# A hybrid decoder layer: residual read back earlier, norm sums in four column quarters, norm factors spread by transposes, attention scores in four quadrants

## What is computed

```python
u = rmsnorm(h, norm1_g);  proj = u @ w_in            # 7 parts of 512 columns
# stick-breaking attention, 8 heads of 64:
z = einsum('bhqd,bhkd->bhqk', qb, k) * scale
log_one_minus = where(visible, log_sigmoid(-z), 0)
later = cumsum(log_one_minus, reverse=True) - log_one_minus
o_sb = where(visible, exp(log_sigmoid(z) + later), 0) @ v
o_sb = group_rmsnorm(o_sb, sb_norm_g, 8)             # mean square over each head's 64
# gated linear recurrence, 4 heads of 128, chunks of 128 tokens
o_hg = hgrn2_chunkwise(q, k, v, log_f)
o_hg = group_rmsnorm(o_hg, hg_norm_g, 4) * silu(g)
h = h + concat([o_sb, o_hg]) @ w_out                 # the residual h is x
ffn = (silu(u2 @ w_gate) * (u2 @ w_up)) @ w_down;  h = h + ffn;  rmsnorm(h)
```

## Time and profile before

| | us |
|---|---|
| median of 3 runs | 1467.88 (1467.37 to 1468.05) |
| the profiled execution's time | 1466.36 |
| its span | 1464.3 |
| TensorE busy | 1401.8 |
| VectorE busy | 738.0 |
| ScalarE busy | 440.6 |

### The profile page before, as it was taken

One profiled execution on the slowest core, in us unless ns is written; L12 is line 12 of the kernel. 1 busy time (PEld: TensorE's weight loads), 2 busy tenths in 40 slices (PEclk: granted clock), 3 DMA queues, 4 the chain that ended last, 5 costly groups with the idle time before them and its releaser, 6 DMA issues.

```text
span 1464.3 us, 20834 instructions
## 1 busy us (share of the span) xinstructions
PE 1401.8 (96%) x8732; PEld 1190.4 (81%) x8732; DVE 738.0 (50%) x1178; ACT 440.6 (30%) x770; POOL 20.3 (1%) x48
## 2 busy tenths in 40 slices
PE   5999999998999999769999999999999999999998
PEld 5898989897777777569987888888888888888886
DVE  6476677763776565812542435252533425152437
ACT  6323322223665556811432112111111112121113
POOL 3000000000000000010000000000000000000000
PEclk9999999999999999989999999999999999999999
DMA  6211111010010000040121011020201111020202
GB/s 189 58 30 30 30 30 53 22 44 0 1 59 1 30 2 30 1 158 30 58 73 58 29 58 58 29 87 0 86 23 63 31 55 57 29 86 0 86 0 115
DMA packets 61194, 68.78 MB, mean 47 GB/s; under 512 B 1584, under 2 KB 54832, under 8 KB 61120
## 3 DMA queue, kind: packets, MB, share of 16 engines
q1 hardware_dynamic: 59408, 61.94, 13.2%
q0 software_dynamic: 1712, 5.78, 1.1%
HBM read 63.51 MB, written 4.19 MB: 46 GB/s over the span
## 4 chain that ended last, share of the span: by engine, by line
PE 91%; ACT 5%; DMA 1%; issue 1%; DVE 1%; POOL 0%; ACTq 0%; DVEq 0%; POOLq 0%
PE ps L268 18%; PE ps L269 18%; PE ps L270 18%; PE ps L1542 16%; PE ps L936 3%; PE ps L917 2%; PE ps L280 2%; PE ps L282 2%; PE ps L281 2%; PE ps L901 2%; PE ps L549 2%; PE ps L384 1%; DMA h_res<-in_x_dram 1%; ACT bv L503 1%; ACT beta L1029 1%
## 5 line engine op out<-in xcount | busy, mean ns | idle before, releaser
L268 PE MATMUL ps<-a_hi,w_hi 128*128 128x512 f32 (+2 forms) x960 | 357.0, 372 | 8.5 <-DVE a_lo L376 2.9
L269 PE MATMUL ps<-a_lo,w_hi 128*128 128x512 f32 (+2 forms) x960 | 349.6, 364 | 0.0
L270 PE MATMUL ps<-a_hi,w_lo 128*128 128x512 f32 (+2 forms) x960 | 349.3, 364 | 0.0
L268 PEld LDWEIGHTS ps<-a_hi,w_hi 128*128 128x128 f32 x960 | 181.4, 189 | 33.8 <-DVE a_lo L376 3.3
L270 PEld LDWEIGHTS ps<-a_hi,w_lo 128*128 128x128 f32 x960 | 181.4, 189 | 23.4
L269 PEld LDWEIGHTS ps<-a_lo,w_hi 128*128 128x128 f32 x960 | 181.6, 189 | 22.1
L1386 DVE TENSOR_TENSOR silu<-silu,ps 128x512 f32<-128x512 f32 x44 | 30.2, 687 | 319.1 <-ACT silu L1272 319.1
L1398 DVE TENSOR_TENSOR h_res<-h_res,ps 128x512 f32<-128x512 f32 x176 | 116.3, 685 | 48.0 <-PE ps L1542 47.9
L1272 ACT ACTIVATE silu<-ps 128x512 f32<-128x512 f32 x44 | 26.4, 600 | 337.2 <-PE ps L270 337.2
L268 PE MATMUL ps<-a_hi,d_hi 128*128 128x512 f32 x320 | 124.5, 389 | 0.0
L269 PE MATMUL ps<-a_lo,d_hi 128*128 128x512 f32 x320 | 124.5, 389 | 0.0
(11 more groups left out here) (193 smaller groups left out, 1959.8 us busy)
## 6 DMA issues: line engine op xcount, KB each, us to landing
w_raw<-in_w_in_dram SPq DMA_DIRECT2D x24, 512.0 KB
w_raw<-in_w_gate_dram SPq DMA_DIRECT2D x11, 1024.0 KB, 5.1
w_raw<-in_w_up_dram SPq DMA_DIRECT2D x11, 1024.0 KB, 5.2
w_raw<-in_w_down_dram SPq DMA_DIRECT2D x11, 1024.0 KB, 5.0
mixed<-in_x_dram SPq DMA_DIRECT2D x8, 512.0 KB, 7.3
w_raw<-in_w_out_dram SPq DMA_DIRECT2D x4, 1024.0 KB
h_res<-in_x_dram POOLq DMA_DIRECT2D x8, 512.0 KB, 8.0
out_dram<-h_sq SPq DMA_DIRECT2D x8, 512.0 KB, 2.6
```

Source lines behind the costliest of these rows:

```text
L268: nc.tensor.matmul(psum, wh, ah, start=k == 0, stop=False)
L269: nc.tensor.matmul(psum, wh, al, start=False, stop=False)
L270: last = nc.tensor.matmul(psum, wl, ah, start=False, stop=k == KT - 1)
```

## The change

Five edits:

- GpSimd's queue issues the eight reads of x into `h_res` as soon as attention's last output is out of PSUM, ahead of the read of the second gain, which waits for the last head norm. Each of the eight reads has a semaphore of its own, and DVE waits for each tile's where it first adds to it.
- The sums of squares are made in four matmuls of 32 output partitions in place of one of 128, for each 128 tokens.
- The spread factors are turned by a transpose in place of a float32 matmul with the identity.
- The scores are made in four matmuls of 64 rows by 64 queries in place of two of 64 rows by 128 queries.
- DVE makes the second copy of the last two pieces too.

```diff
+        QUARTERS = [slice(32 * i, 32 * i + 32) for i in range(4)]
...
         def unit_sums(pe, n):
             pe.wait_ge(h_square.sem, h_square.done(n + 1))
             for c in range(UNIT):
-                last = nc.tensor.matmul(bank(4)[:, 2 * P + c:2 * P + c + 1],
-                                        (kd_nat, scores)[n % 2][:, c * P:(c + 1) * P], ones[:, 0:1],
-                                        start=True, stop=True)
+                for rows in QUARTERS:
+                    last = nc.tensor.matmul(bank(4)[rows, 2 * P + c:2 * P + c + 1],
+                                            (kd_nat, scores)[n % 2][:, c * P + rows.start:c * P + rows.stop],
+                                            ones[:, 0:1], start=True, stop=True)
...
         def unit_spread(pe, n):
-                last = nc.tensor.matmul(bank(1 + n % 2)[:, c * P:(c + 1) * P],
-                                        (kd_nat, scores)[n % 2][:, c * P:(c + 1) * P], ident[:],
-                                        start=True, stop=True)
+                last = nc.tensor.transpose(bank(1 + n % 2)[:, c * P:(c + 1) * P],
+                                           (kd_nat, scores)[n % 2][:, c * P:(c + 1) * P], ident[:])
...
-        SCALAR_COPIES = 3 * PER_PAIR
+        SCALAR_COPIES = range(3 * PER_PAIR, NP - 2)
...
-                for par in range(2):
-                    rows = slice(64 * par, 64 * par + 64)
-                    last = nc.tensor.matmul(bank(2 * par + n % 2, w), bq[rows, kv, b * P:(b + 1) * P],
-                                            bf[rows, kv, lo:hi], start=True, stop=hi < width)
+                for q in KEY_HALVES:
+                    for par in range(2):
+                        rows = slice(64 * par, 64 * par + 64)
+                        last = nc.tensor.matmul(bank(2 * par + n % 2, w)[q],
+                                                bq[rows, kv, b * P + q.start:b * P + q.stop],
+                                                bf[rows, kv, lo:hi], start=True, stop=hi < width)
...
-                if n >= SCALAR_COPIES:
+                if n in SCALAR_COPIES:
...
-                if n < SCALAR_COPIES:
+                if n not in SCALAR_COPIES:
...
+                pool.wait_ge(av_evac.sem, av_evac.done(8))
+                for t in range(TT):
+                    pool.dma_start(h_res[:, t, :], x2[t * P:(t + 1) * P, :]).then_inc(x_back[t].sem, 16)
                 pool.wait_ge(s_mixed.sem, s_mixed.done(8))
                 pool.dma_start(gain[:], norm2_g[0:1, :].to_broadcast([P, D])).then_inc(gain2.sem, 16)
-                pool.wait_ge(av_evac.sem, av_evac.done(8))
-                for t in range(TT):
-                    pool.dma_start(h_res[:, t, :], x2[t * P:(t + 1) * P, :]).then_inc(x_back.sem, 16)
...
                 def add(c, t):
+                    if c == 0:
+                        dve.wait_ge(x_back[t].sem, 16)
                     dve.wait_ge(o_proj.sem, o_proj.done(TT * c + t + 1))
...
-                dve.wait_ge(x_back.sem, 16 * TT)
```

More of the change, by code:

```diff
@@ L317, in hybrid_layer @@
         m_hi, m_lo = signal("m_hi"), signal("m_lo")
-        x_back, gain2, gain3 = signal("x_back"), signal("gain2"), signal("gain3")
+        x_back = [signal(f"x_back{t}") for t in range(TT)]
+        gain2, gain3 = signal("gain2"), signal("gain3")
         o_proj, o_add = signal("o_proj"), signal("o_add")
@@ L964, in head_norm_tensor @@
                 for c in range(UNIT):
-                    last = nc.tensor.matmul(psum[:, 2 * c:2 * c + 2], squares[:, c * P:(c + 1) * P],
-                                            ones_pair[:], start=True, stop=True)
+                    for rows in QUARTERS:
+                        last = nc.tensor.matmul(psum[rows, 2 * c:2 * c + 2],
+                                                squares[:, c * P + rows.start:c * P + rows.stop],
+                                                ones_pair[:], start=True, stop=True)
                 last.then_inc(s_sum.sem, 1)
@@ L970, in head_norm_tensor @@
                 for c in range(UNIT):
-                    last = nc.tensor.matmul(psum[:, c * P:(c + 1) * P], spread[:, c * P:(c + 1) * P], ident[:],
-                                            start=True, stop=True)
+                    last = nc.tensor.transpose(psum[:, c * P:(c + 1) * P], spread[:, c * P:(c + 1) * P], ident[:])
                 last.then_inc(s_spread.sem, 1)
```

## The result

The changed kernel takes 1441.95 us (median of four runs, 1441.82 to 1443.12) against 1467.62 for the kernel before beside it: 0.9827 of it, with a 95% interval of 0.981 to 0.9844. That is 25.7 us less, where 1444.5 and 23.4 less were forecast. The two profiled executions differ by less. That of the changed kernel took 1443.12 us, with a span of 1441.1, and is the longest of its four; that of before took 1466.36 and is one of the shorter, since in 18 later runs the kernel before took 1465.56 to 1471.14. So the two traces differ by 23.2 us where the medians differ by 25.7. The mean granted clock doesn't rank them: it was 0.995 in the changed kernel's longest execution and 0.992 to 0.993 in the three shorter ones.

A forecast was written before the change was run, and what follows sets the result against it. TensorE was taken to bound up to 560 us, mostly ScalarE to 623, then the wait for x; 13.1 + 6.4 + 2.4 + 2.1 - 0.6 = 23.4 us less gave 1443.0 profiled, 1444.5 median, range 1439 to 1453.

The forecast's parts named there:

- The reload: Start of the projection out: TensorE's stop of 10.95 us and 2.19 us of slow clock both go, 13.1 us won.
- The spreads: Spread factors by transposes: 0.46 us saved at each of 14 places in recurrence, first three pairs and projection out, 6.4 us.
- TensorE's saving is the kernel's up to 560 us: Before the last pair of heads, each ns off TensorE's own work should shorten the kernel; TensorE busy 98% and 95%.
- a sign of being wrong in the recurrence: New TensorE wait for VectorE's factors in the recurrence; as a rival up to 4.5 us lost, 1449 us, 8%.
- The sums: Sums of squares in quarters: 0.10 us won nine times, 0.30 five times in attention, 2.4 us together.
- the good bound of the prediction: Sums, if four quarters load at once: 32 records take 0.24 us, +5.6 us; the other bound 0.94 us, -4.2.
- The losses at the change of form: Around each sum: 0.14 us lost going into smaller tiles, 0.20 us back to full width; in attention only 0.14.
- the 60 cycles for 32 records: Skill-page estimate against the sums edit: 60 cycles for each record, 0.80 us a sum, the edit coming to -1.9 us.
- The quadrants: Attention scores in four tiles at once: 0.05 us saved a piece, 42 pieces ahead of ScalarE's stretch, 2.1 us.
- The rival that they go two by two: Attention scores: second 64 queries wait for the first, each pass over keys made twice; 1474 us, slower; 5%.
- The copies: End of attention: VectorE's second copy of the last piece but one some 0.6 us late; -0.6 us, at best 0.
- The last pair: Last pair of heads, 560 to 623 us: waits run mostly through ScalarE, so TensorE's savings count as nothing.

## Why the prediction was right, point by point

**The reload** was right in mechanism and size: 13.1 us forecast, 13.13 measured alone. TensorE's next late partner was nothing, as said, and the first x did land ahead of VectorE. The part that the separate semaphores play is 0.7 us.

**The spreads** were right in mechanism and 10% too large: 0.46 us for each, 0.45 measured in the recurrence and 0.36 in attention. The step that failed is that TensorE's saving is the kernel's up to 560 us: TensorE was busy 98% and 95% there, and still at two of thirteen places all or most of what its records saved was lost again, once to a new wait of 0.52 us for VectorE's head norm, the kind of wait that the prediction named as a sign of being wrong in the recurrence and priced only there.

**The sums** are the term that was mis-sized, at 2.4 us. Measured in 13 of 14 places: 5.4, a little above the good bound of the prediction (5.3 for these, 5.6 for all). Of the two bounds for 32 records I took 0.47 us from between, and they take 0.26, close to the lower bound. I had written that L540 and L549 show no floor yet and still added one. The losses at the change of form were too large in the prediction, 0.34 us for both ways: at 106.20 us before the eight records took 0.81 us to the next group and the stretch from L270 to the second matmul behind 1.21; now the 32 records and one more bunch's distance take 0.29 and the stretch 0.88, so of 0.52 won in the records 0.33 come out and 0.19 are lost. Nor do all sums in the recurrence pay both ways; three pay only the way back.

The Trainium skill (TensorEngine Tiling (Array Packing), sections Key Properties and Instruction Overhead) is half borne out and was half misapplied: a change of mode does cost, some 0.2 us a sum for both ways. But the prediction counted the 60 cycles for 32 records one after another, while Key Properties lets different tiles load and multiply in parallel, and what was split here is the 128 stationary columns, not the side that was small. Each of the four tiles starts a record every 0.03 us or so, which is not sooner than the page's 60 cycles (0.025 us at 2.4 GHz, an estimate from that page), so this case doesn't contradict the least time. (By the prediction's own terms that estimate comes to -2.2 us, not -1.9.)

**The quadrants** were right in mechanism: four tiles at once, in either order, and a piece 0.04 us shorter (0.05 forecast). The kernel sees 0.026 a piece in the first two pairs (0.73 us for 28, and 0.71 in the changed kernel against the one without) and 0.036 in the third, 1.2 us for 42 in place of 2.1. In the profiled execution of the quadrants alone the clock fell in the third pair and took it back. The rival that they go two by two, the only one that would have been slower, fell.

**The copies** cost 0.63 us in the kernel before, as worked out from the earlier trace rows, and nothing in the changed one. The price hung on a margin of 0.4 us between two engines, which the other edits moved. Which of them moved it wasn't tried.

**The last pair** gave nothing or lost a little, as taken: 67.85 us from its first scores to the projection out, 67.72 before.

**The total.** The terms as measured alone are 13.1 + 5.4 + 5.4 + 1.2, and 0.8 for the last half's sums and spread in the projection out: 25.9 together. The 0.8 shows in the kernel without quadrants, which takes 189.06 us from the projection out to the second product where the reload alone takes 189.84. In the changed kernel the same stages, from the first unit to the second product, give 22.3 us. Of the missing 3.6, two falls of the clock where TensorE is the bound are 3.0, which no term held, and 0.5 is the recurrence, where the spreads and sums together win 6.36 us and alone 6.82. Add the 0.9 us of the earlier rise of the clock and the traces' 23.2 are there.

So the forecast of the total is in part luck: 1443.0 was forecast for a profiled execution and 1443.12 measured, because sums that won some 3 us more than forecast were set off by falls of the clock of 3 us. And that the terms come to the medians' 25.7 is no proof to the tenth: the medians of the kernel before were 1466.15, 1466.58, 1467.49 and 1467.62 us in four sets of runs.

## What to carry to other kernels

When an engine stops, look at what its data waits for in the queue, not at how long the transfer is: the reload was over in 14 us either way, and some 12.4 of the 26 us won came from issuing it ahead of a wait that it had nothing to do with. A sum over partitions by a matmul with one column moving is all load of the stationary side, and in column tiles the loads run side by side; even in the middle of full-width work, with the array's form changed ahead and behind, a sum became 0.33 us shorter. Price each place by itself, since the form may have changed there already. Price a small edit on the stretch between two events of one profile, and price it in the kernel that it goes into: 0.6 us in the one were 0 in the other.

## What the hardware showed that I had not expected

Records of 32-column tiles follow each other by 0.008 us on average, in bunches of four tiles some 0.03 us apart. A scan of 400 columns on VectorE goes from 1036 to 1812 ns while GpSimd copies and subtracts. The scan and the product each read two operands from SBUF, for which the Trainium skill (GPSIMD Engine Reference, section Specifications) has VectorE and GpSimd contend for a shared interface, and the trace agrees: beside an idle GpSimd, in the same execution as slow ones, the scan of 512 columns took 1202 ns. The granted clock can drop to the 1.2 GHz level for 3.4 us in attention, in most kernels here, though TensorE's records cover 95% of that stage: just ahead of the fall at 493.5 they covered 1.62 of 3.50 us. Such a fall costs 1.5 us where TensorE is the bound. After the same 1.62 of 3.50 us it came in some kernels and not in others. The runs of the kernel before spread by up to 6 us (1465.10 to 1471.14). What decides the falls stays open.
